# One tile of tokens takes its expert values by gathered rows instead of dense matmuls

## The chip, the cores and the metric

The kernel runs on one core of a Trainium2 chip. The metric is the device time of one launch in microseconds (us), the median of three runs.

## The reference, cut to what matters

The program is a trunk of two layers over 512 tokens of width 1024, in float32: a mixer (layer 0: state-space plus window attention; layer 1: mLSTM), a PEER feed-forward and a gated embedding. The change is in the PEER part, which picks 128 of 16384 experts for each token (8 heads, 16 each) with a gate for each:

```python
def expert_block(args):
    hx, ix, gx = args                        # 128 tokens, their 128 expert indices and gates
    act = jax.nn.gelu(jnp.einsum('tkd,td->tk', u[ix], hx), approximate=False) * gx
    return jnp.einsum('tk,tkd->td', act, v[ix])
```

## The kernel before

Activations lie transposed, features on the 128 partitions and the 512 tokens along the free side. The picked experts are not gathered. Everything is dense: gelu(u h) is computed for all 16384 experts, a dense gate array (zero for what a token did not pick) is multiplied in, and all of v is applied.

**Units.** Every weight comes in units of 128x1024 (512 KB). SP loads unit u into one of four raw slots once unit u-4 is split (`load`, L147). ScalarE rounds it to fp32r (`w_hi`, `split_hi`, L154), VectorE, in some stages GpSimd, forms the rest `w_lo` (L161, L168), and TensorE does 24 matmuls with it (`product`, L175, line 185): 8 tiles of 128 rows, each as hi x hi, hi x lo, lo x hi, 512 columns wide. Split buffers are two deep, so `w_hi` of unit u waits for the matmuls of unit u-2. All engines run one long program without barriers; the order on each is written out by hand.

**Stages of one PEER part.** `TopK` finds the experts while the first units of u are multiplied. `Decode` (16 units) turns positions into key numbers and gates and has TensorE transpose them (L1391). `Gates` has 4 steps of 20 units of u and 128 tokens: for each token VectorE, ScalarE and GpSimd build two one-hot arrays, TensorE multiplies them (L1587, 256 columns), VectorE sums the result to a group of gates (L1516) and GpSimd stores groups of 32 tokens to DRAM. Beside all of these ScalarE applies gelu to each unit's product and stores it to DRAM (`acts`, 128 key rows of 128x512).

**Values.** `Values` starts with a tail of 12 more units of u and then has 16 blocks of 8 units of v, unit j of a block adding into PSUM bank j (1024 features = 8 banks) for the block's 8 key rows. For each block GpSimd loads the 8 rows of activations (`gelu_block`, 2 MB, L1677) and their gates (`gate_block`, 2 MB, L1678) into one of two buffers. In the block ahead of its use, one row in each unit: VectorE multiplies the two (`mult`, L1690), ScalarE rounds (`hi`, L1684), VectorE forms the rest (`lo`, L1702). TensorE waits for `lo` of row k ahead of tile k of the block's first unit. The last block adds PSUM to the residual and begins the norm of the next stage (`Ple`).

**Elsewhere.** The front of layer 0 (`EvenFront`, L399) and its SSD stage load their units one after another on SP; the odd mixer loads 4 units per head (L2015).

Of the kernel before, what the change touches and what calls it, by code (L numbers as in the profile page):

```python
# [25 lines left out]
P = 128  # L26
# [17 lines left out]
TG = 32  # L44
NTG = T // TG
# [60 lines left out]
class Program:  # L106
    def __init__(self, nc, ctx, dram):
# [20 lines left out]
        self.spare = sb("spare", [P, 1])  # L128
        self.ps = ctx.enter_context(nc.psum_tensor("ps", [P, 8, 512], F32))
# [96 lines left out]
def start(p, nxt):  # L226
# [3 lines left out]
    with nc.Block() as block:  # L230
# [28 lines left out]
        def _(pool):  # L259
# [4 lines left out]
                           allow_small_or_imprecise_dtypes=True)  # L264
            nc.gpsimd.memset(p.ident[:, :], 0.0).then_inc(const.sem, 1)
# [8 lines left out]
    ld.base += 16  # L274

# [123 lines left out]
class EvenFront:  # L399
# [8 lines left out]
    def __init__(self, p, b, nxt, ctx):  # L408
# [10 lines left out]
        self.first_keys, self.keys_copied = Mark(p.sig("first_keys_loaded"), 16), Mark(p.sig("keys_copied"), 32)  # L419
# [30 lines left out]
    def sync(self, sp):  # L450
        p, w, u0 = self.p, self.p.dram["ev_in"], self.u0
        tiles = lambda m: m.rearrange("p (k c) -> p k c", c=P)
        for n in range(RAW, len(EV_ORDER)):
            if EV_ORDER[n] == KEYS_AT:
# [8 lines left out]
                continue  # L463
            p.load(sp, u0 + n, (u0 + n) % RAW, w[EV_ORDER[n], :, :])
# [272 lines left out]
class EvenSSD:  # L737
# [8 lines left out]
    def __init__(self, p, b, front, kept, nxt, ctx):  # L746
# [7 lines left out]
                  ("ssd_rows", 1), ("ssd_rows_kept", 16), ("ssd_squares_added", DK - 1))  # L754
# [20 lines left out]
        self.loaded = [Mark(p.sig(f"ssd_row_loaded{r}"), 16 * (H // self.RING)) for r in range(self.RING)]  # L775
# [334 lines left out]
class TopK:  # L1110
# [35 lines left out]
    def sync(self, sp):  # L1146
# [203 lines left out]
class Decode:  # L1350
# [6 lines left out]
    def __init__(self, p, b, rows, us, n0, nxt, ctx):  # L1357
        self.p, self.b, self.rows, self.us, self.n0, self.nxt = p, b, rows, us, n0, nxt
        self.gs, self.gx_, self.dr, self.dt, self.gh = (
# [10 lines left out]
        self.gr = p.sb("gate_rounded", [P, T], F32R, ctx=ctx)  # L1370
# [3 lines left out]
    def sync(self, sp):  # L1374
        p, u0 = self.p, self.u0
        for j in range(RAW, self.N):
            p.load(sp, u0 + j, (u0 + j) % RAW, self.us[self.n0 + j, :, :])
        prefetch(p, sp, self.nxt, u0 + self.N)

    def tensor(self, pe):  # L1380
# [8 lines left out]
        for k in range(3):  # L1389
            for t in range(TT):  # L1390
# [28 lines left out]
    def vector(self, dve):  # L1419
# [29 lines left out]
        dve.sem_inc(self.dr.sem, 1)  # L1449
        dve.wait_ge(self.dt.sem, self.dt.at(1))  # L1450
        v.memset(b["sel"][:, :, T:], 0.0)
        v.tensor_copy(gr[:, :], p.ps[:, 4, :]).then_inc(self.gh.sem, 1)
        v.tensor_copy(b["sel"][:, 0:2, 0:T], p.ps[:, 2:4, :])
        dve.wait_ge(self.gh.sem, self.gh.at(1))
        v.tensor_copy(b["sel"][:, 2, 0:T], gr[:, :].bitcast(F32))
        link(v.tensor_tensor(b["sel"][:, 3, 0:T], p.ps[:, 4, :], gr[:, :].bitcast(F32), ALU.subtract))
        link.done()


class Gates:  # L1460
# [8 lines left out]
    NS = T // TS  # L1469

    def __init__(self, p, b, rows, us, n0, gates, nxt, ctx):
        self.p, self.b, self.rows, self.us, self.n0, self.gates, self.nxt = p, b, rows, us, n0, gates, nxt
        R, R1, NS = self.R, self.R1, self.NS
        self.h1 = Mark(p.sig("hot_first"), T)
        self.h2 = Mark(p.sig("hot_second"), T + self.H0)
        self.hs = Mark(p.sig("hot_scaled"), T + R1)
        self.gm = Mark(p.sig("gate_summed"), T + R)
        self.copied = Mark(p.sig("gate_copied"), T // 4 + 2)
# [72 lines left out]
    def gpsimd(self, pool):  # L1551
# [3 lines left out]
        self.store(pool, 0, NTG + 1)  # L1555
# [16 lines left out]
        self.store(pool, 3, NTG)  # L1572
# [48 lines left out]
class Values:  # L1621


    TAIL = 12
    AHEAD = 4

    def __init__(self, p, b, rows, gate_stage, us, gates, vs, halves, nxt, ctx):
        self.added = Mark(p.sig("values_added"), DK)
        self.after = None
        self.p, self.rows, self.gs, self.us, self.gates, self.vs, self.nxt = p, rows, gate_stage, us, gates, vs, nxt  # L1630
        B = BLOCK
        self.gt_, self.ah = (Mark(p.sig(n), KEYS) for n in ("gated", "act_hi"))
        self.al = Mark(p.sig("act_lo"), KEYS + 2 * B)
        self.bl = (Mark(p.sig("block_loaded0"), 32 * (NBLOCK // 2 - 1)),
                   Mark(p.sig("block_loaded1"), 32 * NBLOCK // 2))
        self.fg, self.fr, self.fs = (Mark(p.sig(n), 16) for n in ("first_gates", "first_rows", "first_rest"))
        self.at = p.sb("gelu_block", [P, 2, B, T], ctx=ctx)
        self.gt = p.sb("gate_block", [P, 2, NTG, B * TG], ctx=ctx)
        self.halves = halves
        self.t0 = p.unit  # L1640
# [11 lines left out]

    def sync(self, sp):
# [9 lines left out]
    def gpsimd(self, pool):  # L1663
        B, at, gt, al, bl = BLOCK, self.at, self.gt, self.al, self.bl
        rows = self.rows.acts.rearrange("n p t -> p n t")
# [8 lines left out]
        def body(i, s, fixed, half):  # L1674
# [5 lines left out]
            if fixed == 0:  # L1680
                self.rows.wait_stored(pool, KEYS)
# [856 lines left out]
```

## Time and profile before

| | |
|---|---|
| time, median of 3 runs | 4242.54 us (4242.18 to 4243.04) |
| profiled execution, span | 4241.3 us (1.2 under the median) |
| TensorE busy / VectorE / ScalarE / GpSimd | 99% / 64% / 49% / 31% |
| value blocks, layer 0 | from 1304 to 1996 us |
| value blocks, layer 1 | from 3476 to 4168 us |
| gate stage, layer 0 | 737 to 1237 us |
| moved by DMA | 657 MB, mean 155 GB/s |

Matmuls overlap in the records, so a matmul's own duration (0.39 us) is longer than the distance between two of them. That distance is read from a count in a stretch. Engine lines with a "q" are queues: SPq is SyncE's instruction queue, where DMAs are issued. "L164 <- ACT" names a wait and what ended it.

### The profile page before, as it was taken

The numbers are of one execution on the slowest core, as the hardware profiler recorded it, in microseconds if no ns is written. First come the engines' busy times: TensorE is split into PE (matmuls) and PEld (weight loads), VectorE is DVE, ScalarE is ACT, GpSimd is POOL, SyncE is SP. The second block draws the span as 40 slices with busy tenths as digits, with TensorE's granted clock in tenths as the row PEclk, the third lists the DMA queues.
The fourth block names the chain that finished last, engine by engine and source line by source line (L and its number), as shares of the span: only waits on it lengthen the run. The fifth ranks groups of instructions, "written<-read, shape, count | busy, mean of one in ns | idle before, by whom it ended". The sixth has DMA issues, their size and how long they took to land.

```text
span 4241.3 us, 61024 instructions
## 1 busy us (share of the span) xinstructions
PE 4178.4 (99%) x19147; PEld 3414.8 (81%) x19147; DVE 2726.4 (64%) x5671; ACT 2068.8 (49%) x4041; POOL 1328.0 (31%) x1650
## 2 busy tenths in 40 slices
PE   8998999999999999999999999999999999999998
PEld 6666888888888888888788888888888888888886
DVE  4647898877764444444777765997777744444445
ACT  3756333877753333334555553336777833333334
POOL 0312446877750000001200002457788810000001
PEclk9999999999999999999999999999999999999999
DMA  3122334555566555653222223335554575655542
GB/s 118 55 68 72 114 119 161 205 183 186 204 249 211 186 205 176 214 176 102 80 85 86 84 88 106 111 132 194 186 206 179 204 276 174 217 173 204 187 139 85
DMA packets 183260, 657.49 MB, mean 155 GB/s; under 512 B 19744, under 2 KB 19872, under 8 KB 178240
## 3 DMA queue, kind: packets, MB, share of 16 engines
q1 hardware_dynamic: 104752, 370.89, 25.7%
q0 software_dynamic: 41488, 217.65, 14.6%
q10 hardware_dynamic: 36864, 67.13, 4.3%
q8 instruction: 67, 1.10, 0.1%
q14 instruction: 89, 0.73, 0.1%
HBM read 510.56 MB, written 144.77 MB: 155 GB/s over the span
## 4 chain that ended last, share of the span: by engine, by line
PE 83%; DVE 6%; ACT 5%; issue 4%; POOL 1%; ACTq 0%; DVEq 0%; POOLq 0%
PE ps L185 76%; PE ps L1587 2%; ACT first_scaled L1606 2%; ACT w_hi L158 1%; DVE od_tmp L371 1%; POOL w_lo L171 1%; DVE w_lo L164 1%; PE ps L1170 1%; PE ps L1860 1%; PE ps L897 0%; PE ps L2086 0%; ACT gelu L1097 0%; PE ps L541 0%; PE ps L542 0%; DVE gate_group L1516 0%
## 5 line engine op out<-in xcount | busy, mean ns | idle before, releaser
L164 DVE TENSOR_TENSOR w_lo<-w_raw,w_hi 128x1024 fp32r<-128x1024 f32 x584 | 719.5, 1232 | 1055.9 <-ACT w_hi L158 1052.1
L158 ACT ACTIVATE w_hi<-w_raw 128x1024 fp32r<-128x1024 f32 x693 | 734.8, 1060 | 1090.3 <-PE ps L185 955.0
L185 PE MATMUL ps<-h_hi,w_hi 128*128 128x512 f32 x3072 | 1210.4, 394 | 20.8 <-DVE h_lo L314 10.5
L185 PE MATMUL ps<-h_hi,w_lo 128*128 128x512 f32 x3072 | 1197.2, 390 | 0.0
L185 PE MATMUL ps<-h_lo,w_hi 128*128 128x512 f32 x3072 | 1196.6, 390 | 0.0
L185 PE MATMUL ps<-y_hi,w_hi 128*128 128x512 f32 x2368 | 926.2, 391 | 2.6 <-POOL w_lo L171 1.7
L185 PE MATMUL ps<-y_hi,w_lo 128*128 128x512 f32 x2368 | 922.8, 390 | 0.0
L185 PE MATMUL ps<-y_lo,w_hi 128*128 128x512 f32 x2368 | 922.6, 390 | 0.0
L1568 POOL TENSOR_SCALAR second_hot<-iota,token_keys 128x128 fp32r<-128x128 f32 x1024 | 722.2, 718 | 0.0
L185 PEld LDWEIGHTS ps<-h_hi,w_hi 128*128 128x128 f32 x3072 | 577.1, 188 | 152.0 <-issue 22.6
L185 PEld LDWEIGHTS ps<-h_hi,w_lo 128*128 128x128 f32 x3072 | 576.8, 188 | 122.3
L185 PEld LDWEIGHTS ps<-h_lo,w_hi 128*128 128x128 f32 x3072 | 577.2, 188 | 116.2 <-issue 2.2
L1606 ACT ACTIVATE first_scaled<-first_hot,token_keys 128x128 fp32r<-128x128 f32 x1792 | 542.5, 390 | 1.5 <-issue 0.9
L185 PEld LDWEIGHTS ps<-y_hi,w_hi 128*128 128x128 f32 x2368 | 445.4, 188 | 95.8 <-POOL w_lo L171 2.5
L185 PEld LDWEIGHTS ps<-y_hi,w_lo 128*128 128x128 f32 x2368 | 444.9, 188 | 93.9
L185 PEld LDWEIGHTS ps<-y_lo,w_hi 128*128 128x128 f32 x2368 | 445.1, 188 | 89.4
L1677 POOL DMA_DIRECT2D gelu_block<-acts x30 | 26.6, 885 | 1187.7 <-DVE y_lo L1704 594.1
L171 POOL TENSOR_TENSOR w_lo<-w_raw,w_hi 128x1024 fp32r<-128x1024 f32 x109 | 284.5, 2610 | 312.8 <-ACT w_hi L158 312.7
L1516 DVE TENSOR_REDUCE gate_group<-ps 128x512 f32<-128x1024 f32 x256 | 302.7, 1216 | 6.1 <-PE ps L1587 6.1
L1537 DVE TENSOR_SCALAR first_hot<-iota,token_keys 128x128 f32<-128x128 f32 x1024 | 242.2, 305 | 90.7 <-PE ps L1587 42.2
L1097 ACT ACTIVATE gelu<-ps 128x512 f32<-128x512 f32 x256 | 150.6, 588 | 172.1 <-PE ps L185 170.3
L1687 ACT ACTIVATE y_hi<-gelu_block 128x512 fp32r<-128x512 f32 x128 | 81.1, 634 | 245.7 <-DVE gelu_block L1699 245.7
(348 smaller groups left out, 3544.8 us busy)
## 6 DMA issues: line engine op xcount, KB each, us to landing
w_raw<-in_u SPq DMA_DIRECT2D x256, 512.0 KB, 3.3
w_raw<-in_v SPq DMA_DIRECT2D x256, 512.0 KB, 3.3
gates<-gate_group POOLq DMA_DIRECT2D x36, 2048.0 KB, 7.9
acts<-gelu ACTq DMA_DIRECT2D x256, 256.0 KB, 2.0
gate_block<-gates POOLq DMA_DIRECT2D x32, 2048.0 KB, 17.9
gelu_block<-acts POOLq DMA_DIRECT2D x30, 2048.0 KB, 11.5
w_raw<-in_od_in SPq DMA_DIRECT2D x65, 512.0 KB, 3.3
w_raw<-in_wq SPq DMA_DIRECT2D x32, 512.0 KB, 3.3
```

What stands on the lines that cost most here:

```text
L158: self.nc.scalar.activation(self.wh[:, slot % SPL, :], self.raw[:, slot, :], ACT.Copy).then_inc(self.sig("w_hi_ready").sem, 1)
L164: self.nc.vector.tensor_tensor(self.wl[:, slot % SPL, :], self.raw[:, slot, :], self.wh[:, slot % SPL, :].bitcast(F32), ALU.subtract).then ...
L171: self.nc.gpsimd.tensor_tensor(self.wl[:, slot % SPL, :], self.raw[:, slot, :], self.wh[:, slot % SPL, :].bitcast(F32), ALU.subtract).then ...
L185: ins = self.nc.tensor.matmul(out, a[:, s, w], b[:, k, :], start=first and j == 0 and m == 0, stop=last and j == n - 1 and m == 2)
L371: ins = v.scalar_tensor_tensor(out=dst[k], in0=src[:, k:k + T], scalar=taps[k], in1=dst[k - 1], op0=ALU.mult, op1=ALU.add)
L1097: p.nc.scalar.activation(self.ga[:, s, :], p.ps[:, s, :], ACT.Gelu).then_inc(self.ge.sem, 1)
L1516: v.tensor_reduce(gb[:, half, :, at:at + 4].rearrange("p a t -> p t a"), self.bank(q).rearrange("p t c a -> p t a c"), AX_X, ALU.add).then ...
L1537: ins = v.tensor_scalar(o1[:, t % R1, :], p.iota[:, :], self.key(0, t), None, ALU.is_equal)
L1568: ins = p.nc.gpsimd.tensor_scalar(self.o2[:, t % self.R, :], p.iota[:, :], self.key(1, t), None, ALU.is_equal)
L1587: ins = p.nc.tensor.matmul(self.bank(q)[:, r, :, :].rearrange("p c a -> p (c a)"), self.o2[:, t, :], self.os[:, t, :, :].rearrange("p c a ...
L1606: ins = p.nc.scalar.activation(self.os[:, t % self.R, c, :], self.o1[:, t % self.R1, :], ACT.Copy, scale=self.key(2 + c, t))
L1687: self.p.nc.scalar.activation(self.halves[s][0][:, j, :], self.at[:, s, j, :], ACT.Copy).then_inc(self.ah.sem, 1)
```

## The change

Of the four tiles of 128 tokens the last one leaves the dense path of gates and values; u and gelu stay dense for all 512 tokens.

- **Copies.** SP copies v to a second DRAM array with one expert per row of 4 KB (`ValueRows`), 128 copies per layer of 1024 pieces of 512 bytes. For layer 0 they stand between the weight loads of the front (two for each load), the SSD stage (four, for 8 loads), TopK and Decode; for layer 1 in the odd mixer (eight per head).
- **Decode** also forms for the last tile, on VectorE, the expert number of each pick and the place of its activation in `acts`, and transposes only three tiles.
- **Gates** has 3 steps (384 tokens), so `Values` has a tail of 32 units of u and not 12.
- **Own.** For pick k = 0 to 127 of each of the 128 tokens GpSimd issues two indirect DMAs: the activation (128 elements of 4 bytes, 24 picks ahead) and the value row (128 rows of 4 KB, ring of four buffers). VectorE multiplies activations by gates (in groups of 16) and adds `row * act` to a sum of 128x1024. The additions stand in blocks 1 to 13, ten a block.
- **Values.** Matmuls, `mult`, `hi`, `lo` are 384 wide. `lo` is on GpSimd. Rows and gates are fetched by SP, one row per unit, two blocks ahead. In the last block TensorE transposes the sum into the free 128 columns of each bank.
- `Ple` takes its buffers from the ring.

```diff
+DT = T - P
+NTD = DT // TG
+class ValueRows:
+    def __init__(self, p, units, rows):
+        self.units = units
+        self.to = rows.rearrange("(i b k) (q d) -> i k b q d", i=NBLOCK, b=BLOCK, q=DK)
...
+    def copy(self, sp, i, q):
+        src = self.units[bass.ds(i * DK + q, 1), :, :].rearrange("o k (b d) -> (o k) b d", b=BLOCK)
+        dst = self.to[bass.ds(i, 1), :, :, q, :].rearrange("o k b d -> (o k) b d")
+        sp.dma_start(dst, src).then_inc(self.done.sem, 16)
...
@@ class OddMixer, sync
             for j in range(4):
                 p.load(sp, i * 4 + h0 + j, (h0 + j) % RAW, w[i * 4 + 1 + j, :, :])
+                for q in (2 * j, 2 * j + 1):
+                    p.value_rows[1].copy(sp, i - 1, q)
...
+class Own:
+    K = PEER_HEADS * SEL
+    GROUP = 16
+    RING = 4
+    LEAD = 24
+    FIRST = 1
+    TURNS = (1, 1, 1, 2, 1, 1, 1, 2)
...
+    def load_act(self, pool, k):
+        if k < self.K:
+            pool.indirect_dma_start(self.act[:, k:k + 1], None, self.acts,
+                                    bass.IndirectOffsetOnAxis(ap=self.act_at[:, k:k + 1], axis=0)
+                                    ).then_inc(self.al[k // self.GROUP % 2].sem, 16)
+    def load_row(self, pool, k):
+        r = k % self.RING
+        if k < self.K:
+            if k >= self.RING:
+                pool.wait_ge(self.used.sem, self.used.at(k - self.RING + 1))
+            pool.indirect_dma_start(self.ring[:, r, :], None, self.rows.rows,
+                                    bass.IndirectOffsetOnAxis(ap=self.row_at[:, k:k + 1], axis=0)
+                                    ).then_inc(self.rl[r].sem, 16)
+    def add(self, dve, link, k):
...
+        r = k % self.RING
+        dve.wait_ge(self.rl[r].sem, self.rl[r].at(16 * (k // self.RING + 1)))
...
+            dve.wait_ge(self.used.sem, self.used.at(k))
+            ins = v.scalar_tensor_tensor(out=self.sum[:, :], in0=self.ring[:, r, :], scalar=self.act[:, k:k + 1],
+                                         in1=self.sum[:, :], op0=ALU.mult, op1=ALU.add)
+        ins.then_inc(self.used.sem, 1)
@@ class Gates
-    NS = T // TS
+    NS = DT // TS
@@ class Values
-    TAIL = 12
+    TAIL = 32
...
     def gpsimd(self, pool):
...
+        for i in range(NBLOCK):
+            s = i % 2
+            for j in range(B):
+                if i == 0:
+                    for k in range(j * per, j * per + per):
+                        own.load_act(pool, k)
+                if j == 0:
+                    self.lo(pool, i, s, B - 1)
+                elif i < NBLOCK - 1:
+                    self.lo(pool, i + 1, 1 - s, j - 1)
+                for k in own.turns(i, j):
+                    own.load_act(pool, k + own.LEAD)
+                    own.load_row(pool, k + own.RING)
...
     def tensor(self, pe):
...
+                ins = p.product(pe, i * B + u0 + j, (u0 + j) % RAW, p.ps[:, j, 0:DT], *self.dense[s],
+                                first=fixed == 0, last=fixed == NBLOCK - 1, wait_tile=tile)
+                if fixed == NBLOCK - 1:
+                    if j == 0:
+                        pe.wait_ge(own.used.sem, own.used.at(own.K))
+                    ins = p.nc.tensor.transpose(p.ps[:, j, DT:T], own.sum[:, j * P:(j + 1) * P], p.ident[:, :])
...
     def vector(self, dve):
...
             for j in range(B):
                 p.split_lo(dve, i * B + u0 + j + 1, (u0 + j + 1) % RAW)
...
+                if i < NBLOCK - 1:
+                    self.mult(dve, i + 1, 1 - s, j)
+                for k in own.turns(i, j):
+                    own.add(dve, link, k)
```

## Rows read from the trace of the kernel before

**Rows 1.** The page: span, busy time of TensorE, and its clock in 40 slices.
```profile
span 4241.3 us, 61024 instructions
PE 4178.4 (99%) x19147; PEld 3414.8 (81%) x19147; DVE 2726.4 (64%) x5671; ACT 2068.8 (49%) x4041; POOL 1328.0 (31%) x1650
...
PEclk9999999999999999999999999999999999999999
```

**Rows 2.** Busy time by stretch: values, gates, start of the tail, front, heads.
```profile
core 0: us, PE busy (x) PEld busy (x) DVE busy (x) ACT busy (x) POOL busy (x), PEclk, DMA share, GB/s
1302.00:1932.00 630.00, 629.74 (x2779) 521.12 (x2778) 281.87 (x348) 197.09 (x233) 28.41 (x28) 1.00 0.55 190
737.00:1237.00 500.00, 497.81 (x2417) 418.06 (x2416) 389.89 (x841) 389.99 (x1048) 395.02 (x643) 1.00 0.54 193
1237.00:1302.00 65.00, 65.00 (x289) 53.81 (x288) 22.91 (x27) 24.00 (x32) 4.86 (x6) 1.00 0.82 303
45.00:215.00 170.00, 168.40 (x806) 122.23 (x805) 100.14 (x170) 95.23 (x220) 39.56 (x32) 1.00 0.21 69
...
2090.00:2520.00 430.00, 428.99 (x2056) 349.94 (x2057) 323.62 (x654) 244.64 (x406) 10.94 (x17) 0.99 0.26 85
```

**Rows 3.** Chain that ended last, in order of time: start, duration, what.
```profile
1304.59 691.86 PE ps L185 x3051
```

**Rows 4.** Groups of TensorE in the gate stretch, 737 to 1237 us.
```profile
L1587 PE MATMUL ps<-first_scaled,second_hot 128*128 128x256 f32 x512 | 74.9, 283 | 1.7 <-DVE gate_group L1516 1.5
```

**Rows 5.** Timeline of TensorE in a head; groups of weight loads.
```profile
2321.54 2.40 PE L2065 MATMUL ps<-v_turned_od,od_w 128*128 128x130 f32 x20
...
L185 PEld LDWEIGHTS ps<-y_hi,w_lo 128*128 128x128 f32 x478 | 89.7, 188 | 18.6
```

**Rows 6.** Groups of VectorE, whole run.
```profile
L164 DVE TENSOR_TENSOR w_lo<-w_raw,w_hi 128x1024 fp32r<-128x1024 f32 x584 | 719.5, 1232 | 1055.9 <-ACT w_hi L158 1052.1 <-ACT q L953 2.6
L1699 DVE TENSOR_TENSOR gelu_block<-gelu_block,gate_block 128x512 f32<-128x512 f32 x256 | 175.4, 686 | 0.0
L314 DVE SCALAR_TENSOR_TENSOR h_lo<-residual,params,h_hi 128x512 fp32r<-128x512 f32 x32 | 23.9, 749 | 14.1 <-ACT h_hi L296 14.1
```

**Rows 7.** Groups of GpSimd, whole run.
```profile
L489 POOL TENSOR_TENSOR conv_sums<-conv_sums,z 128x512 f32<-128x512 f32 x12 | 15.3, 1275 | 0.9
L1678 POOL DMA_DIRECT2D gate_block<-gates x30 | 34.5, 1152 | 0.9 <-issue 0.9
L1677 POOL DMA_DIRECT2D gelu_block<-acts x30 | 26.6, 885 | 1187.7 <-DVE y_lo L1704 594.1 <-DVE h_lo L1704 593.6
L2043 POOL DMA_DIRECT2D od_row<-gates x15 | 8.1, 542 | 369.4 <-DVE od_w L2289 369.4
```

**Rows 8.** Timeline of Decode, 643 to 654 us: VectorE and GpSimd.
```profile
643.07 2.41 POOL L171 TENSOR_TENSOR w_lo<-w_raw,w_hi 128x1024 fp32r<-128x1024 f32 x1 [4.04 <-ACT w_hi L158]
643.26 2.77 DVE L1426 TENSOR_TENSOR gate_terms<-top_sums 128x512 f32<-128x512 f32 x1
...
647.50 4.51 POOL L171 TENSOR_TENSOR w_lo<-w_raw,w_hi 128x1024 fp32r<-128x1024 f32 x1 [2.02 <-ACT w_hi L158]
649.80 4.36 DVE L1440 TENSOR_TENSOR pos_equal<-pos_equal,key_index 128x2048 f32<-128x2048 f32 x1
```

**Rows 9.** Line 461, DMAs of 1024 pieces: issue durations (ns) and landing.
```profile
L461 SPq DMA_DIRECT2D w_raw<-in_ev_in x2: 664/1858/3052, 8.4 to 9.2; - x2
...
DMA to landing us min/median/max: 8.9/8.9/8.9
```

**Rows 10.** Timeline of SP's queue: weight loads of front and SSD stage.
```profile
18.04 195.34 SPq L152 DMA_DIRECT2D w_raw<-in_ev_in  x26
...
222.91 174.95 SPq L152 DMA_DIRECT2D w_raw<-in_ev_out  x16
```

**Rows 11.** DMA issues in the stretch 1237 to 1302 us; the last number is landing.
```profile
w_raw<-in_u SPq DMA_DIRECT2D x7, 512.0 KB, 7.4
...
w_raw<-in_v SPq DMA_DIRECT2D x5, 512.0 KB, 3.3
```

**Rows 12.** Waits: who waited for whom, in total, times, longest.
```profile
DVE selected L1451 <- PE ps L1391: 18.3, 2, 9.1
```

More of the change, by code:

```diff
@@ L1153, in body @@
             p.load(sp, i * 8 + u0 + L + 2 * c + 1, (u0 + L + 2 * c + 1) % RAW, self.wq[i * 4 + c + L, :, :])
+            if self.layer == 0:
+                for q in (2 * c, 2 * c + 1):
+                    p.value_rows[0].copy(sp, i + 11, q)
         self.loop(sp, body)
@@ L1449, in vector @@
         dve.sem_inc(self.dr.sem, 1)
+        mine, own = slice(DT // P * S, TT * S), self.own
+        expert, place = self.expert[:, 0, :], self.expert[:, 1, :]
+        link(v.scalar_tensor_tensor(out=expert, in0=key[:, 0, mine], scalar=float(KEYS), in1=key[:, 1, mine],
+                                    op0=ALU.mult, op1=ALU.add))
+        link(v.scalar_tensor_tensor(out=place, in0=expert, scalar=float(T),
+                                    in1=p.token[:, :].to_broadcast([P, S]), op0=ALU.mult, op1=ALU.add))
@@ L1682, in gpsimd @@
-        self.blocks(pool, body)
+        B, own = BLOCK, self.own
+        pool.wait_ge(own.ready.sem, own.ready.at(1))
+        pool.wait_ge(own.rows.done.sem, own.rows.done.at(16 * KEYS))
+        for k in range(own.RING):
+            own.load_row(pool, k)
+        for j in range(B - 1):
+            self.lo(pool, 0, 0, j)
+        self.rows.wait_stored(pool, KEYS)
+        per = own.LEAD // B
+        for i in range(NBLOCK):
+            s = i % 2
+            for j in range(B):
+                if i == 0:
[8 more added lines that the diff above has]
+                    own.load_row(pool, k + own.RING)
@@ L1810, in load @@
     def load(self, sp):
+        own = self.values.own
+        sp.wait_ge(own.used.sem, own.used.at(own.K))
         sp.dma_start(self.e[:, :, :], self.src).then_inc(self.ld.sem, 16)
@@ L2426, in ffn @@
                 with ExitStack() as c:
-                    topk = TopK(p, b, rows, wq, us, d[f"sub{layer}"], before, hn, firsts(us[n1:]), c)
+                    topk = TopK(p, layer, b, rows, wq, us, d[f"sub{layer}"], before, hn, firsts(us[n1:]), c)
                 with ExitStack() as c:
-                    decode = Decode(p, b, rows, us, n1, firsts(us[n2:]), c)
+                    decode = Decode(p, layer, b, rows, own, us, n1, firsts(us[n2:]), c)
             with ExitStack() as c:
@@ L2433, in ffn @@
             pairs = ((before.hi, before.lo), hn)
-            values = Values(p, b, rows, gates, us, d["gates"], vs, pairs,
+            values = Values(p, b, rows, own, gates, us, d["gates"], vs, pairs,
                             [pw_[0, :, :], pw_[1, :, :], gate[0, :, :], gate[1, :, :]], c)
```

227 lines of the change are left out of this document (142 added, 85 removed).

## The prediction, made before the result was known

> **What bounds the kernel now.** I read the page first: TensorE is busy for 99% of the span and its clock is full [rows 1]. Then the stretches [rows 2] and the chain in order of time [rows 3]. In the stretch 1302 to 1932 us, the value sums of layer 0, the reader is to see PE busy for 629.7 of 630 us, and in the chain one piece of 691.86 us that is nothing but line 185. So a value block costs what its matmuls cost: 2779 in 630 us are 226.7 ns each, 24 make a unit of 5.44 us, 8 units a block of 43.5 us, 16 blocks 696.5 us a layer. VectorE (282 us), ScalarE (197) and GpSimd (28) have room, and the DMA share is 0.55 at 190 GB/s. Only the PE columns are worth anything there.
>
> **Part 1: narrower matmuls.** The line now has 384 columns. By columns alone the spacing is 0.75 x 226.7 = 170 ns. The nearest narrower rows: in the gate stretch 500 us hold 1905 wide matmuls (431.9 us at 226.7) and 512 of 256 columns [rows 4], which leaves 133 ns each, waits included; a line through both gives 180. Matmuls of 130 columns, each with its own weights, stand 112 ns apart [rows 5], so loading weights is no floor at 170. The duration of one load, 188 ns [rows 5], is the upper bound all the same. I take 177: unit 4.25 us, block 34.0 us (bounds 32.6 and 36.1). If nothing else came in the way a layer's values would take 544 us.
>
> **Part 2: one tile less in the gates.** 128 of 512 one-hot matmuls go in each layer, 128 x 133 ns = 17.0 us, 34 us for both (lower bound 14.3 at 112 ns; 17.0 is also the upper one, since the 133 hold the waits). The 20 units of line 185 that stood among them move into the tail of the next stage at the same price, where VectorE and GpSimd have little to do.
>
> **Part 3: the sums on VectorE and the move of `lo` to GpSimd.** Blocks 1 to 13 carry ten additions each (the last one eight); I call them heavy. A 128x1024 addition has two SBUF inputs and a scalar: 749 ns at 512 elements [rows 6], and the 1232 and 686 ns of the tensor-tensor rows give 1.07 ns an element, so 1.30 us. The product at 384 wide is 0.55 us. VectorE per heavy block: 8 x 1.23 + 8 x 0.55 + 10 x 1.30 = 27.2 us. GpSimd's `lo` at 384, from 1.28 us at 512 and 2.40 us at 1024 undisturbed [rows 7, 8], is 0.99 us, 7.9 us a block. ScalarE's `hi` only gets narrower. Alone each fits into 34. But the two exclude each other: w_lo on GpSimd runs from 643.07 for 2.41 us, and a product on VectorE that starts at 643.26 ends only at 646.03, 0.55 us after it; the next w_lo takes 4.51 and VectorE's following product 4.36 [rows 8]. So they add up: 35.1 us, a little over PE's 34.0.
> The Trainium skill ("SBUF — State Buffer", section "Who interferes with whom") says the same and speaks against this change: a VectorE instruction with two SBUF inputs and a GpSimd instruction that reads SBUF block each other outright. By that rule the additions and `lo` cost 35.1 us, by the busy times read engine by engine 27.2; the trace agrees with the rule.
>
> **Part 4: what moves by DMA.** A heavy block loads 4.19 MB of weights, 1.57 of activations, 1.57 of gates and 5.24 of gathered rows, 12.6 MB; before it was 8.4 MB in 43.5 us. The crowded stretch at the start of the stage moved 303 GB/s at a share of 0.82 [rows 2], that is 370 when full: 34.0 us. Then there are 1280 elements of 4 bytes. No row shows such; 1024 pieces of 256 bytes (the pair on line 461, 3.77 us to issue) cost 1.9 us at most [rows 9], so 0 to 2.4 us. DMA therefore wants 34 to 36.4 us of a heavy block, without a gap.
> The Trainium skill ("DMA: Bandwidth & Descriptors", "Specifications") puts the limit of HBM per core near 358 GB/s, which would make it 35.1 us; here single slices of the profile reach more.
>
> **Part 5: GpSimd's issue work.** Per heavy block 20 indirect DMAs. The trace has none. Its plain ones take 542 ns (128 rows), 885 (1024) and 1152 (2048) [rows 7]. An indirect one reads its indices first, and I take 1.0 us, nearest to the middle of these; lower bound 0.54, upper bound open, and I carry it to 2.5 (a GpSimd pass over 1024 elements, 2.4). At 1.0 us: 20 + 7.9 = 27.9 us.
> The order matters more than the sum. `load_row` waits for the addition on VectorE (a new wait) and behind it on GpSimd stands `lo` of the next row, for which TensorE waits. At the end of a block, from the start of its last unit on: VectorE ends its product at 3.0 us, its two additions at 4.3 and 5.6; GpSimd issues its second pair until about 7.0 to 7.8, then `lo` of row 7 to 8.0 to 9.7 us. TensorE reaches that tile at 4.25 + 21 x 0.177 = 8.0 us. So 0 to 1.7 us late per block, and I take 1.0. A heavy block: the highest demand, 36.4, plus 1.0, is 37.4 us (bounds 35.1 and 41.5).
> Sum of a layer's values: 13 x 37.4 + 3 x 34.0 = 588.2 us, plus 8 transposes of 0.11 us (the wait for the sums, at j = 0 of the last block, should be over by then, since the last addition is in block 13): 589.2, which is 107.3 less than 696.5. Both layers: 214.6 us.
>
> **Part 6: the row-wise copies.** 128 per layer, 1024 pieces of 512 bytes, on SP between the weight loads. Each moves 0.52 MB in small pieces; the 256-byte pair took 0.66 and 3.05 us to issue [rows 9]. I take 1.9 us a copy, with a weight load at 0.52 MB / 370 = 1.4 us. Room: the loads of the front stage come every 195.34/26 = 7.5 us [rows 10] with two copies each (5.2 us), in the SSD stage every 10.9 us with four (9.0), in the odd mixer a head lasts 26.9 us with four loads and eight copies (20.8) [rows 2]. The matmuls there hide them, and three units of prefetch cover unevenness. The copies' queue is passed by GpSimd's row broadcasts too, which can land later. I charge 10 us for it all (bounds 0 and 40).
> Decode's five small VectorE operations stand ahead of a wait of 9.1 us per layer for the transposes [rows 12], which hides them; without that cover they would cost about 1 us. Embedding and norm buffers only change place.
>
> **The sum.** The profiled execution spans 4241.3 us [rows 1], 1.2 below the median of the runs. 4241.3 - 214.6 - 34.0 + 10 = 4002.7, so 4004 as timed.
>
> **Rivals.**
> A, all hidden: every resource keeps up with 34.0 us a block. 16 x 34 + 1 = 545 a layer; 4241.3 - 303 - 34 = 3904, timed 3905. For it: VectorE alone is at 27.2. Against: the exclusion in [rows 8] and a DMA demand of a full 34. Chance 0.20.
> D, DMA-bound below its best rate: the 303 GB/s of the crowded stretch make a heavy block 41.5 us, a layer 641.5, the total 4110. For it: weight loads landed in 7.4 us there, against 3.3 otherwise [rows 11]. Against: that stretch had pauses of its own. Chance 0.17.
> B, GpSimd issue-bound, the slower side: at 2.0 us per indirect DMA a heavy block is 7.9 + 40 = 47.9 us, a layer 725.7 with its transposes; 4241.3 + 58.4 - 34 + 10 + 1.2 = 4277. It decides from 1.93 us on, where a heavy block reaches 46.6. For it: nothing in the trace shows the price, and POOL must do it in order with `lo`. Against: plain DMAs of eight times the rows take 0.885. Chance 0.14.
> C, the copies are not hidden: at 4.45 us each (half the 8.9 us of [rows 9]) the front loses 26 x 2.8, the SSD stage 8 x 8.3, the odd mixer 15 x 14.3, together 353 us: 4347. It decides from 3.9 us a copy. Against: 8.9 us was the landing of both behind a crowd of first loads. Chance 0.05.
>
> **Chances.** My forecast 0.42, with 3955 to 4060 as its own range; A 0.20, D 0.17, B 0.14, C 0.05, the rest scattered. The range runs from just under A to between D and B: 3895 to 4180. Faster by over 0.2% (8.5 us, what a measurement here can tell): forecast, A, D and the milder part of B, 0.81; within 0.2%: 0.03; slower 0.16.
>
> **What would show it.** In the profile after: line 185 at 384 columns spaced 170 to 188 ns in block 0 and the last two, where no addition runs (part 1); PE waits in blocks 1 to 13, released by GpSimd's `lo` (ordering), by w_lo (shared reads) or by w_raw loads landing over 10 us late (DMA), and few in the others; `lo` on GpSimd of 1.0 us alone and up to 2.3 beside an addition (part 3); the indirect DMA's own duration (part 5, rival B from 1.93); weight loads in the front, SSD and odd stages released as before (part 6). The forecast is wrong if heavy blocks come out under 35 or over 41.5 us, or if the stretches outside the values grow by more than 40 us.

## The result, and the profile after

4144.88 us, the median of 4 runs (4143.09 to 4150.11), against 4242.52 before on the same chip: ratio 0.9772, 95% interval 0.9758 to 0.9786. It is faster by 97.6 us; 238 were forecast. The time lies in the wide range of the prediction (3895 to 4180) and outside the forecast's own (3955 to 4060).

The page of the kernel after shows TensorE no longer busy throughout, its clock below 1.0 in some value slices, and a chain with 15% on GpSimd. That share alone proves nothing: the page of e5, where TensorE is busy for 98%, has 16% there. The waits further down decide.

```profile
span 4148.4 us, 60526 instructions
PE 3915.3 (94%) x18901; PEld 3361.0 (81%) x18901; DVE 2879.2 (69%) x5309; ACT 1898.0 (46%) x3593; POOL 2012.7 (49%) x2025
...
PEclk9999999999999989999999999999999999889899
...
PE 70%; POOL 15%; issue 6%; DVE 4%; ACT 4%; DMA 0%; ACTq 0%; DVEq 0%; POOLq 0%
```

**Where the time went by stage.** Starts and ends are those of the first matmuls of blocks and stages in the trace. Values of layer 0: 696.9 us before, 662.8 after; layer 1: 696.9 and 668.0. That is 63.0 us gained, 214.6 were forecast. From the first one-hot matmul of a gate stage to the first value matmul it is 17.3 and 16.8 us less, as forecast. What lies ahead of the gates of layer 0 is 2.8 us longer in this trace (it varies by 4.7 us between the traces of the kernels below), all the rest together 1.5. So what is missing, 151.6 us, is missing in the value blocks:

| us | block 0 | 1 | 2 to 10 | 11 | 12 | 13 | 14 | 15 |
|---|---|---|---|---|---|---|---|---|
| after, layer 0 | 39.8 | 40.8 | 42.8 to 44.4 | 42.2 | 39.6 | 38.2 | 33.3 | 34.2 |

A block without additions and gathers costs 33.3, a crowded one 44. Inside blocks 1 to 11, the crowded ones, the eight units take 11.83, 5.93 and then 4.16 to 4.61 us (means of layer 0): most of the loss sits in the first unit, where TensorE needs `lo`.

The busy times of 400 us of crowded blocks and of the whole stage of layer 0 (for the stage before: [rows 2]):

```profile
core 0: us, PE busy (x) PEld busy (x) DVE busy (x) ACT busy (x) POOL busy (x), PEclk, DMA share, GB/s
1400.00:1800.00 400.00, 336.13 (x1766) 324.64 (x1765) 297.44 (x245) 113.12 (x148) 325.33 (x255) 0.90 0.87 287
...
1284.80:1947.60 662.80, 576.76 (x3081) 562.26 (x3080) 466.53 (x399) 203.02 (x264) 477.07 (x380) 0.92 0.80 266
```

TensorE is idle for 86.0 us of the stage. What it waited for in the 400 us (total, times, longest) is GpSimd's `lo` for 60.9 of 63.9 us:

```profile
PE ps L188 <- POOL h_lo L1854: 33.8, 10, 6.5
...
PE ps L188 <- POOL y_lo L1854: 27.1, 8, 6.3
```

It is busy for 576.8, although the same matmuls take 534 when nothing disturbs them (16 blocks of 33.3 us, and 0.9 for the transposes): 42 us more. Most of that, some 32 us by the spacing of the matmuls, stems from the granted clock, 0.92 on the mean; the rest is delays shorter than a matmul's record, which count as busy. One boundary shows the wait and the clock. First the chain up to it, in order of time (start, duration, what):

```profile
1543.85 1.76 POOL own_act L1546
1545.61 0.30 issue
1545.91 1.34 POOL own_rows L1556
1547.26 0.30 issue
1547.56 0.94 POOL own_act L1546
1548.51 0.30 issue
1548.81 0.95 POOL own_rows L1556
1549.76 0.02 issue
1549.77 1.02 POOL y_lo L1854
```

Then TensorE's timeline from there (start, duration):

```profile
1550.83 0.69 PE L188 MATMUL ps<-y_hi,w_hi 128*128 128x384 f32 x1 [6.29 <-POOL y_lo L1854]
1551.32 0.53 PE L188 MATMUL ps<-y_lo,w_hi 128*128 128x384 f32 x1
1551.64 0.53 PE L188 MATMUL ps<-y_hi,w_lo 128*128 128x384 f32 x1
...
1555.80 0.36 PE L188 MATMUL ps<-y_hi,w_hi 128*128 128x384 f32 x1
1556.00 0.34 PE L188 MATMUL ps<-y_lo,w_hi 128*128 128x384 f32 x1
```

And the same 5 us by stretch; the 0.50 is the granted clock:

```profile
1550.80:1555.80 5.00, 4.97 (x16) 4.97 (x16) 2.51 (x3) 1.08 (x2) 4.38 (x4) 0.50 0.90 310
```

GpSimd issues four gathers in a row (the two picks of the last unit) and only then forms the last `lo`; TensorE waits 6.29 us for it. Afterwards its matmuls start every 0.32 us, not every 0.173: half clock, 1.2 GHz for 2.4, for nearly 5 us. The Trainium skill ("TensorE: Matmul & The Clock Gate", "Part 1: The HAM clock gate") says that an idle TensorE falls to the lower of two clocks and that activity lifts it again; the trace agrees, 0.53 us for a matmul behind the wait and 0.34 later.

Per crowded block of 44.1 us this makes 33.3 of matmuls, 7.0 idle (63.9 us of idle time in 400 us, 9.07 blocks) and a remainder of 3.8. By the spacing of the matmuls in blocks 2 to 10, 2.5 us of the remainder fall on matmuls at the lower clock and 1.1 on short delays at full clock.

GpSimd and VectorE in the same 400 us, by groups (busy, mean ns, idle time before):

```profile
L1546 POOL DMA_INDIRECT own_act<-acts,own_act_at x89 | 134.0, 1505 | 16.5 <-issue 15.4
L1556 POOL DMA_INDIRECT own_rows<-value_rows,own_row_at x92 | 112.0, 1218 | 56.2 <-DVE own_sum L1574 34.0 <-issue 22.1
L1854 POOL TENSOR_TENSOR y_lo<-gelu_block,y_hi 128x384 fp32r<-128x384 f32 x38 | 40.8, 1074 | 0.7
...
L167 DVE TENSOR_TENSOR w_lo<-w_raw,w_hi 128x1024 fp32r<-128x1024 f32 x73 | 145.8, 1997 | 100.6 <-ACT w_hi L161 90.2 <-issue 10.1
L1574 DVE SCALAR_TENSOR_TENSOR own_sum<-own_rows,own_act,own_sum 128x1024 f32<-128x1024 f32 x92 | 121.4, 1319 | 2.0
```

For one block (divided by 9.07) GpSimd is busy 35.9 us, spends 4.1 in gaps (0.30 between two gathers that follow each other, 0.15 behind a `lo`), and waits 3.7 for additions: 43.7 of 44.1. It has become the engine that sets the pace, with TensorE waiting at the block's boundary.

### The profile page after: what moved, and what is told of

It is laid out like the page before. It is cut to its first block, busy times and chain, and to the rows that moved or that the text cites. A ratio compares the mean times of both kernels' runs of the same rounds, so it can differ in the third digit from the quotient of the medians.

```text
span 4148.4 us, 60526 instructions
## 1 busy us (share of the span) xinstructions
PE 3915.3 (94%) x18901; PEld 3361.0 (81%) x18901; DVE 2879.2 (69%) x5309; ACT 1898.0 (46%) x3593; POOL 2012.7 (49%) x2025
## 4 chain that ended last, share of the span: by engine, by line
PE 70%; POOL 15%; issue 6%; DVE 4%; ACT 4%; DMA 0%; ACTq 0%; DVEq 0%; POOLq 0%
PE ps L188 62%; POOL own_act L1546 6%; POOL own_rows L1556 5%; PE ps L1706 2%; DVE own_sum L1574 2%; POOL h_lo L1854 2%; POOL y_lo L1854 2%; ACT first_scaled L1725 1%; ACT w_hi L161 1%; POOL w_lo L174 1%; PE ps L2243 1%; PE ps L2222 1%; DVE gelu_block L1849 1%; PE ps L1208 1%; PE ps L2013 1%
## 5 line engine op out<-in xcount | busy, mean ns | idle before, releaser
L188 PE MATMUL ps<-h_hi,w_hi 128*128 128x512 f32 (+1 forms) x3072 | 1174.3, 382 | 106.7 <-POOL h_lo L1854 84.0
L188 PE MATMUL ps<-h_hi,w_lo 128*128 128x512 f32 (+1 forms) x3072 | 1155.0, 376 | 0.0
L188 PE MATMUL ps<-h_lo,w_hi 128*128 128x512 f32 (+1 forms) x3072 | 1154.4, 376 | 0.0
L188 PE MATMUL ps<-y_hi,w_hi 128*128 128x512 f32 (+1 forms) x2368 | 890.9, 376 | 88.4 <-POOL y_lo L1854 82.8
L188 PE MATMUL ps<-y_lo,w_hi 128*128 128x512 f32 (+1 forms) x2368 | 881.2, 372 | 0.0
L188 PE MATMUL ps<-y_hi,w_lo 128*128 128x512 f32 (+1 forms) x2368 | 881.0, 372 | 0.0
L1687 POOL TENSOR_SCALAR second_hot<-iota,token_keys 128x128 fp32r<-128x128 f32 x768 | 542.3, 720 | 0.0
L1556 POOL DMA_INDIRECT own_rows<-value_rows,own_row_at x256 | 315.7, 1233 | 199.9 <-DVE own_sum L1574 141.4
L1546 POOL DMA_INDIRECT own_act<-acts,own_act_at x256 | 367.6, 1436 | 59.2 <-issue 48.0
L1574 DVE SCALAR_TENSOR_TENSOR own_sum<-own_rows,own_act,own_sum 128x1024 f32<-128x1024 f32 x254 | 342.5, 1349 | 5.5
```

Source lines behind the costliest of these rows:

```text
L188: ins = self.nc.tensor.matmul(out, a[:, s, w], b[:, k, :], start=first and j == 0 and m == 0, stop=last and j == n - 1 and m == 2)
L1546: pool.indirect_dma_start(self.act[:, k:k + 1], None, self.acts, bass.IndirectOffsetOnAxis(ap=self.act_at[:, k:k + 1], axis=0)).then_inc(s ...
L1556: pool.indirect_dma_start(self.ring[:, r, :], None, self.rows.rows, bass.IndirectOffsetOnAxis(ap=self.row_at[:, k:k + 1], axis=0)).then_in ...
L1574: ins = v.scalar_tensor_tensor(out=self.sum[:, :], in0=self.ring[:, r, :], scalar=self.act[:, k:k + 1], in1=self.sum[:, :], op0=ALU.mult, ...
L1687: ins = p.nc.gpsimd.tensor_scalar(self.o2[:, t % self.R, :], p.iota[:, :], self.key(1, t), None, ALU.is_equal)
```

## The experiments

Eleven kernels. Q is the theory that `lo` comes late because it stands in GpSimd's queue behind the gathers and their waits; P puts it on the exclusion between VectorE and GpSimd; D on DMA. Times are medians; "heavy" is the mean of blocks 1 to 11 of layer 0 (43.4 us in the changed kernel).

| kernel | us | ratio to before | block 0 | heavy | layer 0 |
|---|---|---|---|---|---|
| changed kernel | 4144.9 | 0.9772 (0.9758 to 0.9786) | 39.8 | 43.4 | 662.8 |
| e1 `lo` on VectorE | 3938.1 | 0.9286 (0.9270 to 0.9301) | 52.6 | 34.1 | 561.8 |
| e2 no activations gathered | 4007.0 | 0.9445 (0.9429 to 0.9461) | 34.3 | 37.6 | 593.7 |
| e3 no gathers, no additions | 3887.9 | 0.9165 (0.9149 to 0.9180) | 34.3 | 33.3 | 534.4 |
| e4 no copies | 4144.9 | 0.9768 (0.9751 to 0.9784) | 39.9 | 43.5 | 663.5 |
| e5 e1 with waits in block 0 | 3901.7 | 0.9202 (0.9186 to 0.9217) | 33.9 | 34.0 | 541.5 |
| e6 e1 without activations | 3885.1 | 0.9160 (0.9145 to 0.9175) | 33.9 | 33.3 | 534.3 |
| e7 last unit free | 4073.4 | 0.9601 (0.9585 to 0.9617) | 39.7 | 41.0 | 628.2 |
| e8 additions of one column | 4019.3 | 0.9473 (0.9458 to 0.9489) | 39.5 | 38.8 | 600.3 |
| e9 e5 with its first wait only | 3903.4 | 0.9201 (0.9185 to 0.9216) | 33.9 | 34.1 | 542.6 |
| e10 e9, a unit later | 3905.3 | 0.9208 (0.9192 to 0.9223) | 33.9 | 34.2 | 544.4 |
| e11 e5 with LEAD 16 | 3994.4 | 0.9419 (0.9403 to 0.9434) | 33.9 | 37.1 | 584.2 |

**e1: `lo` goes back to VectorE**, in the order of the kernel before; GpSimd only gathers.

```diff
@@ class Values, gpsimd
-                if j == 0:
-                    self.lo(pool, i, s, B - 1)
-                elif i < NBLOCK - 1:
-                    self.lo(pool, i + 1, 1 - s, j - 1)
@@ vector
+                if j == 0:
+                    self.lo(dve, i, s, B - 1)
                 if i < NBLOCK - 1:
                     self.mult(dve, i + 1, 1 - s, j)
+                    if j:
+                        self.lo(dve, i + 1, 1 - s, j - 1)
```

> Edit: only `lo` goes back from GpSimd to VectorE; gathers, additions and narrow matmuls stay. After the change a heavy block takes 44 us where 37.4 was forecast; the kernel takes 4145 us. Theory Q (GpSimd's queue, in order: 20 indirect DMAs of 1.34 us and 8 `lo` of 1.08 with gaps are 40 us, and TensorE waits for the last `lo` of a block behind them): GpSimd keeps 20 x (1.3 + 0.3) = 32 us and TensorE no longer waits for it; VectorE has 31.6. Heavy blocks fall to 34 to 37 us, the whole to 3940 (3900 to 3970). Theory P (the shared SBUF reads: everything that VectorE and GpSimd do there adds up, indirect DMAs included: 31.6 + 19): heavy blocks stay at 44 or grow to 50, the whole 4145 or more. Theory D (DMA bandwidth): heavy blocks stay at 42 to 44, the whole 4110 to 4145.

3938.1 us: 206.8 less than the changed kernel. Heavy blocks fall from 43.4 to 34.1 with the same gathers, bytes and additions. What cost them 9.3 us was `lo` on GpSimd, and neither the bytes and pieces of DMA nor the additions alone. VectorE's `w_lo` is at 1224 ns again and not at 1997. The edit therefore takes away two things, `lo`'s place behind the gathers and its exclusion with `w_lo`, and no run separates them; TensorE's own waits name `lo` (60.9 of 63.9 us above) and hardly `w_lo` (2.2). Block 0 got worse, 52.6 and 48.9 us; e5 takes that up.

**e2: no activations are gathered** (gates stand in for them).

```diff
     def load_act(self, pool, k):
-        if k < self.K:
+        if False:
```

> Left out: the gather of activations (the 4-byte elements); the additions weigh rows by the gate alone, so that this tile's values are not the reference's. `lo` stays on GpSimd. Q: GpSimd has 10 x (1.23 + 0.3) + 8.6 = 24 us a heavy block, TensorE's 33.3 us decide: heavy blocks 33.5 to 36, the whole 3885 to 3950. P: 27.2 + 8.6 + 9.5 = 45, no change from 44, the whole near 4145. D with bytes as the limit (the elements are 0.05% of them): no change, 4145; D with the number of pieces as the limit: 3950 to 4050.

4007.0, outside the range: half of the indirect DMAs are gone, and heavy blocks still take 37.6. GpSimd now has time (237.6 us busy of 400), but it spends it waiting in the wrong place:

```profile
L1556 POOL DMA_INDIRECT own_rows<-value_rows,own_row_at x102 | 147.4, 1445 | 158.5 <-DVE own_sum L1574 148.3 <-issue 8.0
```

148.3 us it waits for additions with `lo` behind the waiting instruction. Of the 9.3 us between the changed kernel's block and e1's, halving the gathers gives 5.8; 3.5 stay, for the order and its wait, even at half the work. The time lies in the range that the expectation gave to D with the number of pieces as the limit (3950 to 4050). e1 rules that reading out: all pieces move there, in blocks of 34.1. And e6, which gathers as little as e2 but has `lo` on VectorE, has blocks of 33.3.

**e3: the narrower matmuls alone**, no gathers and no additions.

```diff
     def turns(self, i, j):
...
-        return range(first, min(first + self.TURNS[j], self.K)) if i >= self.FIRST else ()
+        return ()
...
-        for k in range(own.RING):
-            own.load_row(pool, k)
```

> Left out: the 128 gathers of rows and of activations and the additions, so the last tile gets no values. Row-wise copies, narrow matmuls, `lo` on GpSimd and the shorter gate stage stay. All theories: every block 33.3 us, 534 a layer, the whole 4145 - 263 = 3882 (3870 to 3895). If blocks take over 34 us the bound lies in `lo` on GpSimd or in the fetches by SP and not in what Own adds.

3887.9, 534.4 and 535.1 us a layer, `lo` still on GpSimd: the floor of the change. Alone there, `lo` costs at most the 1.0 and 1.7 us that block 0 has over 33.3 (34.3 and 35.0), and VectorE's `w_lo` takes 1226 ns.

**e4: the row-wise copies are left out**, the gathers read the same addresses of an array that holds other values.

```diff
     def copy(self, sp, i, q):
-        sp.dma_start(dst, src).then_inc(self.done.sem, 16)
+        pass
```

> Left out: the 256 copies to the row-wise array; rows are gathered from v as it lies (4 KB pieces at the same indices, so the same bytes by number but not the right values). My step on the copies charged 10 us (0 to 40). From the two traces the stretches outside values and gates have not grown: I expect 4145 - 0 to 5. Rival (the copies cost where they stand, hidden by a gain elsewhere): 4105 to 4135. Gathers in the values themselves are the same.

4144.9, the same as with them (4141.1 to 4145.8 for 4143.1 to 4150.1). 256 copies (landing after 6.0 us each) are hidden, as far as these runs can tell.

**e5: waits for block 0's gathers.** In e1 GpSimd has no `lo` between its gathers, and the first 24 gathers of activations run back to back. e5 was meant to spread them over the units.

```diff
                 if i == 0:
+                    pool.wait_ge(self.ah.sem, B + self.ah.base + j + 1)
                     for k in range(j * per, j * per + per):
                         own.load_act(pool, k)
```

> `lo` on VectorE as in e1, and in block 0 GpSimd issues its three gathers of activations per unit only when ScalarE has rounded that unit's row (one wait more), instead of 24 back to back. Theory S (the small gathers, issued in a row, hold up the weight loads in block 0; e1 lost 35 us in its two blocks 0): block 0 falls from 52.6 and 48.9 to about 36 us, the rest stays at 34, time 3905 to 3915. Rival (block 0's loss is the stage's start itself: prefetch and gathered rows that arrive together): nothing moves, 3935 to 3941.

3901.7, 36.4 us less than e1: with e9 the best of the kernels that leave nothing out, 5.9% under the changed one. Block 0 falls from 52.6 to 33.9. In e1 ScalarE waited long for two weight units; its `w_hi` in block 0 ("remote" is read as the landing of the load):

```profile
1309.12 1.06 ACT L161 ACTIVATE w_hi<-w_raw 128x1024 fp32r<-128x1024 f32 x1 [8.53 <-remote]
...
1324.09 1.06 ACT L161 ACTIVATE w_hi<-w_raw 128x1024 fp32r<-128x1024 f32 x1 [11.63 <-remote]
```

SyncE had issued their loads at 1287.73 and 1291.76, 21 and 32 us earlier, where [rows 11] have 3.3 to 7.4. The last gather of the run was issued at 1320.06. DMA was far from busy, in 20 us of e1 and then of e5:

```profile
1300.00:1320.00 20.00, 11.64 (x49) 10.11 (x47) 2.66 (x5) 2.11 (x3) 15.18 (x16) 0.82 0.32 96
```

```profile
1300.00:1320.00 20.00, 20.00 (x117) 20.00 (x117) 10.07 (x15) 7.73 (x10) 15.43 (x16) 1.00 0.62 199
```

But GpSimd issues 16 gathers in both. The bytes were not what came late. Here are the GB/s of e1 in 40 slices from 1296 to 1332 us:

```profile
GB/s 319 344 381 319 335 319 306 329 132 32 0 1 1 0 1 1 0 0 127 228 240 197 11 1 1 0 0 1 1 0 0 0 0 0 0 146 379 276 55 223
```

By the packet records the loads issued up to then have moved as much by 1303 us as in e5, and SyncE's queue moves no packet from 1304.9 to 1312.6 us and from 1316.0 to 1327.6. Yet `w_hi` goes on only at 1309.12 and 1324.09, the second some 19 us after the last packet that can be its own. TensorE is slow too, with nothing in the profile that it waits for: from 1318.29 to 1323.92 its matmuls start 1.41 us apart:

```profile
1321.11 0.68 PE L188 MATMUL ps<-y_hi,w_lo 128*128 128x384 f32 x1 [0.93 <-issue]
1322.52 0.48 PE L188 MATMUL ps<-y_hi,w_hi 128*128 128x384 f32 x1 [0.74 <-issue]
```

So it is not the loads alone that stall beside this run of gathers; GpSimd itself goes on, a gather every 1.25 us. In e5's trace only the first wait holds at all, the other seven are over when GpSimd reaches them. The expectation's reason, the spacing, was therefore in doubt although its time was missed by only 3 us, and e9 to e11 take it up.

**e6: `lo` on VectorE and no activations gathered**, e1 and e2 together.

> `lo` on VectorE as in e1, and no activations are gathered (gates stand in for them; the output differs). Theory S: block 0 at 33.3 to 34, time 3890 to 3900. Rival (DMA bytes and VectorE's load keep the heavy blocks over 33.3 and block 0 slow): 3920 to 3938, since the bytes of the gathered rows are unchanged.

3885.1, five under the range of theory S; every block 33.3 to 34.2. This is as fast as e3: gathered rows (5.2 MB a block) and all additions cost nothing, although DMA is full (376 GB/s at a share of 1.02 in blocks 2 to 10). So what e5 has over it, 16.6 us, comes with the gathers of 4-byte elements, and block 0's loss in e1 did too. Whether they cost by their DMA or by GpSimd's time, which they halve when they go, this run does not say.

**e7: no pick in a block's last unit.**

```diff
-    TURNS = (1, 1, 1, 2, 1, 1, 1, 2)
+    TURNS = (2, 2, 1, 2, 1, 1, 1, 0)
```

> The changed kernel with the same ten additions a block, but none in a block's last unit (turns 2,2,1,2,1,1,1,0 for 1,1,1,2,1,1,1,2), so that `lo` of row 7 stands behind no gather of that unit. Theory O (only the order at the block's boundary makes TensorE wait): TensorE's first unit waits some 4 us less, heavy blocks 39.5 to 41, time 4050 to 4090. Theory L (GpSimd is full: 20 gathers at 1.6 us with the gap and 8 `lo` at 1.1 are 41 us, and port waits add to it): heavy blocks stay at 42.5 to 44, time 4120 to 4145.

4073.4, within the range of O and out of that of L. The boundary eases (first unit 8.5 us for 11.8, where O said some 4 less), but heavy blocks stay at 41.0, and a new wait appears in the fifth unit (5.9 us for 4.2) since the early units are fuller. Order gives back 71 us of the 243 that separate the changed kernel from e5. It is part of the cause and not the whole.

**e8: each addition works on one column**; gathers, `lo` and order are untouched.

```diff
-            ins = v.scalar_tensor_tensor(out=self.sum[:, :], in0=self.ring[:, r, :], ...
+            ins = v.scalar_tensor_tensor(out=self.sum[:, 0:1], in0=self.ring[:, r, 0:1], ...
```

> The changed kernel with all its gathers in place and in order, but each addition works on one column of 1024 (the output differs): VectorE's load and the exclusion beside the gathers go, GpSimd's instructions and the DMA bytes stay. Theory P (the gathers are slow because VectorE's two-input additions hold the port): a gather takes 0.95 to 1.0 us, GpSimd's heavy block is 20 x 1.25 + 8 x 1.0 = 33 us, heavy blocks 34 to 36, time 3905 to 3970. Theory L (the gathers cost what they cost, 1.3 us and the gap, whatever VectorE does): heavy blocks over 40, time over 4070.

4019.3, between both. By groups in 400 us of e8:

```profile
L1556 POOL DMA_INDIRECT own_rows<-value_rows,own_row_at x106 | 124.2, 1171 | 63.5 <-DVE own_sum L1574 38.8 <-issue 24.6
L1546 POOL DMA_INDIRECT own_act<-acts,own_act_at x86 | 107.2, 1247 | 16.2 <-issue 16.2
...
L167 DVE TENSOR_TENSOR w_lo<-w_raw,w_hi 128x1024 fp32r<-128x1024 f32 x85 | 125.8, 1480 | 178.8 <-ACT w_hi L161 178.8
```

These 400 us reach into blocks 12 and 13, which gather no activations. In blocks 2 to 10 alone the activation gathers take 1236 ns (1494 in the changed kernel) and the rows 1240 (1202, so not less), since `w_lo` and the products are still there. GpSimd's block is then 24.8 us of gathers, 8.2 of `lo`, 4.7 of gaps and 1.1 of waits for additions, 38.8 in all and as measured: it still sets the pace. Neither theory was right alone: the additions make 4.6 of the 9.3 us, by longer activation gathers (2.6 us a block) and by GpSimd's waits for them (3.8 before, 1.1 now), but without them GpSimd is still over 33.3.

**e9: e5 with the first of its eight waits only.**

```diff
-                    pool.wait_ge(self.ah.sem, B + self.ah.base + j + 1)
+                    if j == 0:
+                        pool.wait_ge(self.ah.sem, B + self.ah.base + 1)
```

> e5 without seven of its eight waits: GpSimd waits only before its first gather of block 0, then issues all 24 without a wait. In e5's trace the other seven waits never held: its gathers stand 1.25 to 1.66 us apart without a pause, as in e1, and only the first comes 1.6 us later against TensorE. Theory T (it is the moment of the start that decides; the later waits do nothing): as e5, block 0 at 34, 3898 to 3911 us. Theory S (spacing by units prevents the stall): as e1, block 0 near 50, 3930 to 3941 us.

3903.4, within e5's spread (3898.4 to 3910.7). Theory S falls: 24 gathers may run back to back. They only have to start later. Against the first matmul of block 0 they start at 4.0 us in layer 0 and 5.1 in layer 1 in e1, and at 5.9 in both layers in e5 and e9; 0.8 us decide in layer 1.

**e10: the same wait, for the second unit's row.**

```diff
-                        pool.wait_ge(self.ah.sem, B + self.ah.base + 1)
+                        pool.wait_ge(self.ah.sem, B + self.ah.base + 2)
```

> As e9, but the one wait is for the row of the second unit, so that the 24 gathers start about 4 us later still. Theory T in the form that any start behind the first loads of the block will do: block 0 at 34 to 36, 3898 to 3915 us. If only e9's moment happens to be good (the stall depends on where in the stream of loads the run of gathers begins): block 0 over 40 again, 3920 us or more.

3905.3, block 0 at 33.9 in both layers. So it is not one lucky moment; of the starts tried, only the earliest (e1) brings the stall. The start is at 9.4 and 9.1 us here. It costs block 2 1.7 and 2.8 us against e9.

**e11: LEAD 16 for 24** in e5, two gathers of activations a unit in block 0.

```diff
-    LEAD = 24
+    LEAD = 16
```

> e5 with LEAD 16 for 24, two gathers of activations a unit in block 0, so that each unit has a real pause of about 1.5 us and the waits hold. Theory S: block 0 at 33.3 to 34; and a group's last gather comes only one pick ahead of its use, which can cost 0.5 to 1 us every 16 picks. 3895 to 3915 us. If the total of small gathers ahead of the block mattered and not the pause, the same time; if block 0's 0.6 us over 33.3 in e5 is theirs, it goes.

3994.4, a miss by 80 us. Block 0 is as in e5, and a new wait fills seven later blocks of a layer, those in or behind which a group of 16 begins (39.3 to 42.2 us in layer 0, the others 33.3 to 34.2). The waits of VectorE in 400 us of e11 (total, times, longest):

```profile
DVE own_act L1567 <- DMA own_act<-acts,own_act_at: 40.5, 6, 8.5
```

VectorE waits 6.8 us (40.5 / 6) for a group's last gather, which is issued one pick ahead, and `w_lo` stands behind that wait. From the issue of that gather to VectorE's use of the group it is 5.4 to 6.7 us in these blocks. The 8 picks that LEAD 24 adds are no luxury.

## Why the prediction was wrong, point by point

**Part 1, narrower matmuls: right.** 173 ns spacing (177 taken), unit 4.16 us (4.25), a quiet block 33.3 (34.0).

**Part 2, gates: right.** 17.3 and 16.8 us a layer from the first one-hot matmul to the first value matmul, 17.0 forecast.

**Part 3, durations: right.** The addition took 1.27 us undisturbed (1.30), `mult` 0.54 (0.55), `lo` 1.01 (0.99). The exclusion of [rows 8] is there: `w_lo` 1997 ns beside `lo`, 1224 without it. VectorE's block, 297.4 / 9.07 = 32.8 us, is near the 35.1 of the sum, in which all of `lo` was added to VectorE's 27.2.

**Part 4, DMA: the demand was too high.** e5 moves a heavy block in 34.0 us and e6 in 33.3, where 36.4 was taken; the 34.0 at 370 GB/s was right, the addition for the small elements was not needed. The page of e5 has slices of 372 to 376 GB/s. The Trainium skill ("DMA: Bandwidth & Descriptors", "Specifications") puts the limit of HBM per core near 358 GB/s, a stack's 716 divided by two cores. The trace, with one core running, does not agree with it as a limit. DMA was not the highest demand of the kernel that was run, but e5 and e6 have their DMA full (shares of 1.01 and 1.02 in blocks 2 to 10).

**Part 5 failed, and the prediction with it.** It took 1.0 us for an indirect DMA and made GpSimd's block 20 + 7.9 = 27.9 us, well under DMA's 36.4. Measured: 1.36 us on the mean in the crowded stretch (1505 and 1218 ns), so 20 x 1.36 + 8 x 1.09 = 35.9, and 4.1 of gaps make 40.0; 3.7 of waits for additions come on top. This was the largest demand of the block. The price lay inside the bounds (0.54 to 2.5) that the prediction had itself, but the 41.5 that it gave as a heavy block's upper bound did not use them, and the gap was in none of its terms. "At the end of a block ... I take 1.0" was the second half of the failure. The order was described rightly, four issues ahead of `lo` of row 7, but their price was not, and it was assumed that GpSimd comes to the last unit on time. With a demand above TensorE's it comes late, TensorE idles 7.0 us a block and then loses 2.5 at the lower clock and 1.1 in short delays, terms the sum did not have. The mechanism is that of rival B in a milder form. B was priced only at 2.0 us, and its 1.93 is the price at which the gain over the kernel before is gone. By the prediction's own sum GpSimd passes DMA's 36.4 from (36.4 - 7.9) / 20 = 1.43 us on, and that value was not worked out.

Rival D came nearest by number (4110, heavy blocks of 41.5), and that is luck: e1 moves the same bytes and pieces in blocks of 34.1. Rival A's 3905 is what e5 reaches with `lo` on VectorE; A was wrong for the kernel as changed.

**Block 0** was taken as light at 34.0 and cost 39.8 and 41.2. TensorE waits 4.8 and 5.9 us there, again for `lo` of row 7: in GpSimd's queue it stands behind the first three gathers of activations, and these wait 3.8 us (layer 0) for the last store of activations to land.

**Part 6, copies: right in kind.** 10 us were charged, none can be seen in the times (e4).

Sum: values short of the forecast by 214.6 - 63.0 = 151.6 us, gates as forecast (34.2 for 34.0), and all other stretches 4.2 longer where 10 were charged: 151.6 - 0.2 - 5.8 = 145.6. The profiled span fell by 92.9 for the 238.6 expected of it, 145.7 short.

**Shown** is that `lo` on GpSimd beside the gathers is the cause (e1: -206.8 us), that work, order and VectorE's activity each bear a part (e2, e7, e8), and that the copies bear none (e4). The parts overlap and can't be added: from heavy blocks of 43.4, e2 takes 5.8, e7 2.5, e8 4.6, e1 9.3. **Open** is how much of e1's 9.3 is the exclusion of `lo` and `w_lo` and not the queue. Open is also why ScalarE and TensorE stall beside the gathers of 4-byte elements in e1 and not in e5, e9 and e10: the moment of their start decides (e9), but what the late landings and TensorE's slow matmuls have in common was not found.

## What to carry to other kernels

Don't put an operation that TensorE waits for behind indirect DMAs in GpSimd's queue, still less behind one that waits itself. Price such a DMA with its gap and in the company it will have (here 0.95 + 0.30 us alone, 1.36 + 0.30 beside a busy VectorE), and where the engine's demand nears TensorE's, count each stall of TensorE with the slow matmuls behind it (here 2.5 us for 7.0 idle). And look at a stage's first units by themselves: one wait ahead of the first gather was worth 35 us.

## What was not expected of the hardware

- **A gather waits out the VectorE operation that runs when it starts.** Counted from the records of the changed kernel, with tensor-tensor and scalar-tensor-tensor operations: the 191 gathers that start while none of these runs took 0.95 us (0.94 to 0.96, the middle nine tenths), also where one begins later. The 321 that start while one runs took 1.56 on the mean. Where more than 0.3 us of that operation is left (289 gathers), the gather takes this rest and 0.83 us more (0.82 to 0.84). VectorE doesn't pay: in e5 GpSimd does little but gather in the value stage, and `w_lo` takes 1223 ns and an addition 1281. From the timeline of e5, where the second gather starts 0.28 us ahead of an addition's end and takes 1.09:

```profile
1520.53 1.83 POOL L1556 DMA_INDIRECT own_rows<-value_rows,own_row_at  x1 [0.30 <-issue]
1522.66 1.09 POOL L1546 DMA_INDIRECT own_act<-acts,own_act_at  x1 [0.31 <-issue]
```

```profile
1520.27 2.67 DVE L1574 SCALAR_TENSOR_TENSOR own_sum<-own_rows,own_act,own_sum 128x1024 f32<-128x1024 f32 x2
1522.85 1.22 DVE L167 TENSOR_TENSOR w_lo<-w_raw,w_hi 128x1024 fp32r<-128x1024 f32 x1
```

  The Trainium skill ("SBUF — State Buffer", "Who interferes with whom") reports that a tensor-tensor operation was not seen to stall DMAs issued by GpSimd. For these indirect DMAs the traces here say otherwise. Their index list lies in SBUF, which would explain it; that is inferred and was not tested.
- **A gather of 128 elements of 4 bytes costs as much issue time as one of 128 rows of 4 KB**, 0.95 us alone. Taking the small ones out of e1 brought heavy blocks from 34.1 to 33.3, whereas the rows cost nothing (e6); what the 0.8 us are was not tested.
- **Beside a run of small gathers other engines can stall with DMA idle**: in e1 ScalarE sees a landing some 19 us after the load's last packet, and TensorE's matmuls start 1.41 us apart. e1 lost 19.3 and 15.6 us so in its two blocks 0, and nothing like it when the same run began 1.9 and 0.8 us later in the block (e5, e9).
- **The landing of a gather of 4-byte elements is slow** when DMA is busy: 5.4 to 6.7 us from issue to use in e11, where it was exposed, for a transfer of 512 bytes. The row gathers, 0.52 MB each, land after 7.0 us there.
